# Routing of an expert mixture: the sample group's share moved one unit ahead, router gain and norm factor folded elsewhere, expert weights held back for the stores

## What is computed

```python
def rms_norm(x, g):
    xf = x.astype(F32)
    y = xf * lax.rsqrt(jnp.mean(xf * xf, axis=-1, keepdims=True) + NORM_EPS)
    return (y * g.astype(F32)).astype(x.dtype)

def expert_choice_moe(h, router_w, w_gate, w_up, w_down):
    n_tok = B * S
    cap = EC_CAPACITY * n_tok // N_EXPERTS
    xt = h.reshape(n_tok, D)
    aff = jax.nn.softmax((xt @ router_w).astype(F32), axis=-1)
    gates, idx = lax.top_k(aff.T, cap)
    xe = xt[idx]
    hid = jax.nn.silu(jnp.einsum('ecd,edf->ecf', xe, w_gate)) * jnp.einsum('ecd,edf->ecf', xe, w_up)
    ye = jnp.einsum('ecf,efd->ecd', hid, w_down) * gates[..., None].astype(h.dtype)
    y = jnp.zeros((n_tok, D), h.dtype).at[idx.reshape(-1)].add(ye.reshape(-1, D))
# in trunk, per layer:
    h = h + expert_choice_moe(rms_norm(h, ffn_norm[i]), router_w[i], ...)
```

## Time and profile before

| | |
|---|---|
| median of the runs | 2458.11 us |
| the profiled execution: time, span | 2456.45 us, 2454.8 us |
| TensorE busy, mean granted clock | 2367.5 us (96%), 0.985 |
| VectorE busy, ScalarE busy, GpSimd busy | 1742.6 (71%), 1337.0 (54%), 298.8 (12%) |
| experts' weight splits, 128x2048 | ScalarE 1913 ns, VectorE 2289 ns, 384 each |
| load of a chunk of `ret_w_in`, `ret_w_out`, 1 MB | 5.2, 5.1 us to landing |
| DMA rate in the slices of the experts | 389 to 395 GB/s |

### The profile page before, as it was taken

The page is one execution under the profiler, slowest core; times in us unless marked ns, Lnnn a source line. Parts: engine busy times, 40 slices in busy tenths (PEclk is TensorE's granted clock), DMA queues, the critical chain, the costliest instruction groups (busy, mean ns, idle before and its releaser), DMA issues.

```text
span 2454.8 us, 33887 instructions
## 1 busy us (share of the span) xinstructions
PE 2367.5 (96%) x11934; PEld 1934.6 (79%) x11934; DVE 1742.6 (71%) x1989; ACT 1337.0 (54%) x1454; POOL 298.8 (12%) x360
## 2 busy tenths in 40 slices
PE   8999999999979999999999999998889999999997
PEld 6878788687768888888878888886678888888876
DVE  6545455344679888888866677766578888888854
ACT  4223222222447777777764455444157777777762
POOL 1000000000111221112111101000111111121011
PEclk9999999999989999999999999998889999999999
DMA  6424324132499999999972533332599999999931
GB/s 235 132 72 126 108 96 149 59 107 72 157 345 395 389 392 392 394 389 390 388 193 56 134 102 99 93 93 73 170 339 393 392 394 390 389 392 392 356 125 43
DMA packets 210961, 577.27 MB, mean 235 GB/s; under 512 B 24384, under 2 KB 65856, under 8 KB 210752
## 3 DMA queue, kind: packets, MB, share of 16 engines
q1 hardware_dynamic: 193584, 526.35, 57.5%
q0 software_dynamic: 17296, 49.83, 8.0%
HBM read 547.80 MB, written 30.43 MB: 236 GB/s over the span
## 4 chain that ended last, share of the span: by engine, by line
PE 91%; DVE 3%; DMA 3%; issue 1%; ACT 1%; POOL 0%; SPq 0%; DVEq 0%; POOLq 0%; ACTq 0%
PE bank L1557 43%; PE bank L1443 38%; PE bank L1372 4%; PE bank L1380 4%; PE bank L1743 1%; PE bank L1725 1%; DMA rows_normed<-xn_late 1%; DVE d_parts L613 1%; DMA m_x<-rows_normed,idx_t 1%; DMA resid<-in_x_sample 0%; DMA rows_summed<-m_y,idx_out 0%; DMA raw<-in_ret_w_in 0%; DVE top_i L1946 0%; DVE m_at L1948 0%; DMA resid<-rows_summed 0%
## 5 line engine op out<-in xcount | busy, mean ns | idle before, releaser
L2080 DVE TENSOR_TENSOR w_parts<-wt,w_parts 128x2048 fp32r<-128x2048 f32 x384 | 874.5, 2289 | 133.7 <-ACT w_parts L1133 125.3
L1133 ACT CAST w_parts<-wt 128x2048 fp32r<-128x2048 f32 x384 | 734.2, 1913 | 195.0 <-PE bank L1557 184.4
L1557 PE MATMUL bank<-w_parts,m_xt 128*128 128x512 f32 x2976 | 689.0, 390 | 2.1 <-ACT m_y L1191 2.1
L1557 PEld LDWEIGHTS bank<-w_parts,m_xt 128*128 128x128 f32 x2976 | 556.1, 188 | 117.2 <-issue 2.9
L1443 PE MATMUL bank<-d_parts,xt 128*128 128x512 f32 (+1 forms) x1872 | 388.0, 364 | 4.4 <-DVE d_parts L613 4.4
L1557 PE MATMUL bank<-w_parts,m_hidt 128*128 128x512 f32 x1632 | 382.7, 394 | 2.8 <-DVE m_hidt L2072 2.8
L1443 PEld LDWEIGHTS bank<-d_parts,xt 128*128 128x128 f32 x1872 | 316.0, 190 | 62.3 <-issue 7.4
L1557 PEld LDWEIGHTS bank<-w_parts,m_hidt 128*128 128x128 f32 x1632 | 306.1, 189 | 66.0 <-issue 3.3
L604 ACT CAST d_parts<-raw 128x512 fp32r<-128x512 f32 (+1 forms) x168 | 183.3, 1107 | 245.5 <-PE bank L1443 237.4
L613 DVE TENSOR_TENSOR d_parts<-raw,d_parts 128x512 fp32r<-128x512 f32 (+1 forms) x168 | 215.5, 1296 | 134.8 <-ACT d_parts L604 134.3
L1443 PE MATMUL bank<-xt,d_parts 128*128 128x256 f32 (+1 forms) x1536 | 284.1, 340 | 7.0 <-DVE xt L1803 2.9
(11 more groups left out here) (184 smaller groups left out, 2035.6 us busy)
## 6 DMA issues: line engine op xcount, KB each, us to landing
wt<-in_exp_w_gate SPq DMA_DIRECT2D x128, 1024.0 KB, 14.2
wt<-in_exp_w_up SPq DMA_DIRECT2D x128, 1024.0 KB, 13.1
wt<-in_exp_w_down SPq DMA_DIRECT2D x128, 1024.0 KB, 13.3
raw<-in_ret_w_in SPq DMA_DIRECT2D x32, 1024.0 KB, 5.2
raw<-in_na_w_in SPq DMA_DIRECT2D x24, 1024.0 KB, 5.4
raw<-in_ret_w_in SPq DMA_DIRECT2D x32, 512.0 KB, 4.5
raw<-in_ret_w_out SPq DMA_DIRECT2D x16, 1024.0 KB, 5.1
raw<-in_ple_w_gate SPq DMA_DIRECT2D x8, 1024.0 KB, 8.1
```

The costliest lines, as they stand in the source:

```text
L1133: nc.scalar.copy(w_parts[c % RING][:, 0, :], wt[:, place // 2, place % 2 * 2048:place % 2 * 2048 + 2048])\
L1557: last = nc.tensor.matmul(b[:, :], lhs[x][:, 2 * k + j, :], w[:, part, j, f * HALF:(f + 1) * HALF], start=(k == j == 0 and x == part == 0) ...
L2080: v.tensor_tensor(w_parts[c % RING][:, 1, :], wt[:, k // 2, k % 2 * 2048:k % 2 * 2048 + 2048], w_parts[c % RING][:, 0, :].bitcast(F32), AL ...
```

## The change

1. The units end (2,S) (3,S) (3,P) (2,P), so that the last two are prompt units, and a fifth strip is needed (`strips`). All that the sample's routing had in the last unit now lies in the first of the two (`ROUTED`), except `scaled` of its tiles and most of `eight_best`, which are spread over both.
2. The router's columns are transposed from `resid` instead of the normed rows (`norm_columns`, `added_up`). The gain is multiplied into the router's weights once (`rw_gain`, `rw_scaled`), and the row's norm factor is applied as the scale of the exponential (one call for each tile instead of one for each group). `scaled` is still made, for the rows that experts gather, but later.
3. High and low part of the router's weights lie side by side (32 columns), so that two products per tile of the width give all four combinations, 16 products instead of 24. The sum of the two halves is made when they are brought back into tiles, by a product with `two`, two identity matrices above one another.
4. `moe_loads` waits before chunk 6 for the prompt's stores of normed rows too.
5. `keep_busy` of 20 now stands ahead of the prompt's router products in both layers. In layer 1 the order of output products and routing is another, and so are places in memory.

The diff, cut:

```diff
-UNITS = [(0, 0), (0, 1), (1, 0), (1, 1), (2, 0), (2, 1), (3, 1), (3, 0)]
+UNITS = [(0, 0), (0, 1), (1, 0), (1, 1), (2, 1), (3, 1), (3, 0), (2, 0)]
 LAST = len(UNITS) - 1
+ROUTED = LAST - 1
...
+def strips(u):
+    return sum(new_head(k) for k in range(u + 1))
...
-OUT_ORDER = ["out20", "out30", "out21", "out31", "out40", "norm2", "out41", "norm3", "out50", "norm4", "out51", "out00",
-             "norm5", "out10", "lg1", "out01", "lt1", "aff1", "out11", "norm0", "norm1"]
+OUT_ORDER = ["out20", "out30", "out21", "out31", "out40", "norm2", "out41", "norm3", "out50", "out51", "norm4", "norm5",
+             "out00", "lg1", "lt1", "out10", "aff1", "out01", "out11", "norm0", "norm1"]
...
+        def added_up(eng, n, t):
+            for f in range(2):
+                if n == 1:
+                    drained(eng, "ret", ("out", LAST, t, f) if t < 2 else ("out", ROUTED - 1, t - 2, f))
+                else:
+                    drained(eng, "naout", ("out", t, f))
...
+                    sp.dma_start(rw_gain[:].rearrange("p l t -> p (l t)"), ffn_columns).then_inc(late_in, 16)
...
                     if c == 6:
                         sp.wait_ge(sample_out[l], 16 * 4)
+                        sp.wait_ge(rows_out[l], 16 * 2)
...
+            nc.gpsimd.tensor_tensor(two[:, :], ident[0:2 * EXPERTS, 0:EXPERTS], ident[0:2 * EXPERTS, EXPERTS:2 * EXPERTS],
+                                    ALU.add).then_inc(ident_set, 1)
...
             for u in range(len(UNITS)):
-                if u == LAST:
+                if u == ROUTED:
                     for t in GROUP_TILES[1]:
                         root(1, t)
+                if u == LAST:
                     stored_group(0, 1)
...
             def exponents(l, g):
+                n = 1 + 3 * l
                 act.wait_ge(moe_sub[l], 2 - g)
-                x = m_lg[l][:, GROUP_TILES[g][0]:GROUP_TILES[g][-1] + 1, :]
-                nc.scalar.activation(x, x, ACT.Exp).then_inc(moe_exp[l], 1)
+                act.wait_ge(norm_rs[n], nth(n, GROUP_TILES[g][-1]))
+                for t in GROUP_TILES[g]:
+                    nc.scalar.activation(m_lg[l][:, t, :], m_lg[l][:, t, :], ACT.Exp, scale=rstd[:, t:t + 1])\
+                        .then_inc(moe_exp[l], 1)
...
             for t in range(2):
+                norm_high(1, t)
+            for t in range(2):
                 squares(1, t)
-            for t in range(2):
-                norm_high(1, t)
...
             def norm_columns(n, tiles):
                 for t in tiles:
-                    pe.wait_ge(norm_rows[n], nth(n, t))
+                    if n == 0:
+                        pe.wait_ge(norm_rows[n], nth(n, t))
+                    else:
+                        added_up(pe, n, t)
+                    rows = normed(n, t) if n == 0 else resid[:, t, :]
...
-                part_products([rw_parts[k][:, l, :, :] for k in range(2)], lambda k, m, j: xt[k][:, j, first:first + n],
-                              route_phase(l, g), [("lg", g)], DT, lambda m: slice(0, EXPERTS), True, True, m=EXPERTS)
+                for j in range(DT):
+                    for k in range(2):
+                        last = nc.tensor.matmul(b[0:2 * EXPERTS, 0:n], rw_parts[:, l, j, :], xt[k][:, j, first:first + n],
+                                                start=(j == k == 0), stop=(j == DT - 1 and k == 1))
...
-                    last = nc.tensor.transpose(b[:, k * EXPERTS:(k + 1) * EXPERTS], m_at[l][g][:, k * P:(k + 1) * P],
-                                               ident[0:EXPERTS, 0:EXPERTS])
+                    last = nc.tensor.matmul(b[:, k * EXPERTS:(k + 1) * EXPERTS], m_at[l][g][:, k * P:(k + 1) * P],
+                                            two[:, :], start=True, stop=True)
...
             def mixture(l):
+                keep_busy(f"route{l}", ("lg", 0), 20)
                 logits(l, 0)
...
-            keep_busy("route0", ("n1", 0, 0), 20)
             norm_columns(1, (0, 1))
...
```

198 lines of the change are left out of this document (109 added, 89 removed).

## The result

| | before | after |
|---|---|---|
| median of the runs made together | 2458.44 us (2456.77 to 2460.53) | 2463.18 us (2457.17 to 2466.88) |
| ratio, 95% interval | | 1.002 (1.0011 to 1.0029) |
| the profiled execution: time, span | 2456.45, 2454.8 us | 2466.88, 2465.2 us |
| TensorE busy, mean granted clock | 2367.5 us (96%), 0.985 | 2369.6 us (96%), 0.984 |

The changed kernel is slower by 4.7 us, 0.2% of the time. Mind the two profiled executions: that of before is on the fast side of its runs, that of after is the slowest of its own, so the spans differ by 10.4 us where the medians differ by 4.7. The same file run and profiled again (e1) has a span of 2463.0.

The account below looks back on a forecast made before the run. TensorE, busy 96%, was taken as the bound, with VectorE never idle in the routings. Layer 0 +6.3 -3.2, layer 1 -2.8 -3.1, together -2.8: 2455.3 us, range 2446 to 2463 (the forecast's own 2452 to 2459).

Parts of the forecast that it names:

- The sign of the whole: Whole kernel: faster, with layer 0 at +3.1 us and layer 1 at -5.9, together -2.8 us.
- What bounds the kernel: Retention: TensorE waits for almost nothing, so added work shows once TensorE waits; in both routings VectorE is never idle.
- Part 1, the four waits: Layer 0's prompt pair: TensorE waits at o0 0.4, o1 1.75, v0 2.15 and the gate 2.05 us.
- The 8 products: Layer 0 before T: 8 of 24 router products removed, worth -1.8 us.
- Part 1, the clock: Layer 0's prompt pair: only the gate's pause drops the granted clock, +1.7 us; bounds 0 and 8.
- my rival, four falls: Layer 0's prompt pair: the clock falls in all four pauses, +6 us, 2461.3, or 2463 with late gathers; chance 0.13.
- T of layer 0: End of layer 0's last output product (T): 6.3 us later, from waits less removed products +4.6 and clock +1.7.
- Part 2: Layer 0 from T, the last output product's end, to M, the first expert product: 31.8 us, a gain of 3.2.
- The gather under the held chunks: Both routings: the gather meets weight chunks 6 to 9, held for the prompt's stores; +3.3 us each.
- The first rival: Both routings: the gather isn't slowed by the held chunks, -3.3 us twice, 2448.7 us; chance 0.27.
- Part 3 ahead of T: Layer 1 before T: 8 products -1.8, affinities' wait of 1.65 gone, tile products' wait +0.67; sum -2.8 us.
- Part 3 behind T: Layer 1, T to M: indices at T+22.7, store wait gone by itself, M at T+36.6, a gain of 3.1 us.

Follow-up runs that it names:

- e3: Changed kernel with VectorE's order altered in layer 0's last two units, no eight_best ahead of o0's split or between centred and gated; 2457.89 us, 1.0000.
- e5: Changed kernel with the fifth strip, for the last prompt unit, worked out for 384 columns and not 896; 2459.93 us, 1.0008.
- e9: Changed kernel with the unit order of before, all of the sample's routing in the last unit; 2457.41 us, 0.9994.
- e2: Changed kernel without the wait for the prompt's stores ahead of weight chunk 6; 2464.34 us, 1.0026.
- e6: Changed kernel with layer 1's prompt stores sent from SP, one transfer for each grid row of a tile; 2464.08 us, 1.0019.
- e12: Changed kernel with the filling transposes of e11 alone, 102 ahead of the gathered rows and 11 ahead of the first expert product; 2457.18 us, 0.9997.
- e7: Changed kernel with the edits of e3, e5 and e6 together; 2458.12 us, 0.9998.
- e8: e7 with 80 instead of 36 filling transposes ahead of the gathered rows in each layer; 2457.93 us, 0.9995.
- e11: e7 with 102 filling transposes ahead of the gathered rows and 11 more before the first expert product; 2449.92 us, 0.9966.
- e4: Kernel before with the hold alone, chunks 6 to 9 waiting for the prompt's stores of normed rows; 2459.3 us, 1.0005.
- e10: e9 with layer 1's prompt stores sent row by row as in e6; 2455.8 us, 0.9988.
- e13: Kernel before with filling transposes, 66 in layer 0, 86 in layer 1, and 11 ahead of the first expert product; 2454.33 us, 0.9987.

## Why the prediction was wrong

**The sign of the whole is wrong, by two mis-sized terms and one left out.** The sum had one fall of the clock in the prompt pair, and there were two; it had layer 1's last store landing ahead of the indices, and it landed behind them; and it had nothing for the tile products with `two`. Point by point.

- *What bounds the kernel.* Right: each change of VectorE's list in the prompt pair moved T (e3, e5, e9).
- *Part 1, the four waits.* Right in place and order, and 0.75 too small in sum. Idle times of 0.20, 1.46, 1.82 and 2.78 us stand in the rows above. Counted as the forecast counted them, from start to start, they are 0.37 (6.20 for 5.83), 1.75 and 2.11 (7.20 and 7.56 for 5.45), and 2.86 at the gate (679.46 less the end of the gates at 674.05, less the 2.55 of the earlier trace rows). That is 7.1, where 0.4, 1.75, 2.15 and 2.05 were forecast, 6.35. The pause at the gate itself came as worked out (2.78, for 29.8 - 26.95 = 2.85); the 0.8 more lies in the transposes behind it, 2.6 us for 1.7, with the clock down. The 8 products gave 1.85.
- *Part 1, the clock.* **This term failed.** I wrote that the pauses up to 2.15 us "may escape", and took one fall at 1.7. The size of a fall was right: 12.8 and 12.9 us for 48 products, where e5 and e9 took 11.2 and 11.3. But the pause of 1.82 at v0 made the clock fall as well, so there were two falls, 3.2 us for 1.7. It was not chance, for it fell in all six profiles with 1.8 us at v0 (after, e1, e2, e3, e6, e12), and in none with 0.3 (e5, e7, e8, e11). The earlier trace rows had both kinds, a fall after 2.05 us at 1764 and none after 2.07 at 686, and I followed the kinder one. Of my rival, four falls, two happened. That its time, 2461.3 to 2463, lies by the measured 2463.2 is luck: the rest of the way to that time came from the stores and the tile products.
- *Part 1, left out.* The tile products with the matrix `two` contract over 32 rows instead of 16 and take 1.06 us for the sample's tiles, where the kernel before took 0.42: +0.65 in each layer. I had only asked whether they would wait.
- *T of layer 0.* 4.6 + 1.7 forecast. Measured, 7.1 + 3.2 + 0.65 - 1.85 = 9.1 of the 9.3 us by which T is later behind the third group; e9 puts the spread alone at 10.5. The other 0.7 of the 10.0 is the start of that execution: 1.3 us later, of which 0.55 was made up ahead of the third group.
- *Part 2.* The router started at T+5.8, as forecast. The indices, forecast for T+18.4, were there at T+19.0 (T+24.9 before). The last store landed at T+19.5, not T+17, 11.2 us after its issue; the gather went out at T+20.4 for T+19.5, and some 0.5 of that is the wait for the store, for in before it followed the indices by 1.0. It took 9.8 us for 9.4. M is at T+33.1 for T+31.8.
- *The gather under the held chunks.* Right: 9.8 and 10.2 us in after, 9.7 and 9.8 in e1, 8.2 and 10.5 in e4; without the hold 6.0 in layer 1 and 8.4 in layer 0 (e2). The first rival, a gather that isn't slowed, is refuted. What the text cited of the Trainium skill (DMA: Bandwidth & Descriptors, the section on queues, rings and completion order) holds all the same: the two queues took turns packet by packet, and got half each. From 720 to 721 us of after's trace, while the gather (q0) and a weight chunk (q1) moved:

```profile
q0 software_dynamic: 36, 0.15, 50.2%
q1 hardware_dynamic: 36, 0.15, 49.7%
```

What failed was my estimate of 1 us from it, for it left out when the gather's data starts. In e2's layer 1, alone, its first bytes moved 3.6 us after its issue and it landed 2.4 us later; in after's layer 0, 6.3 us after its issue and 3.4 later. So half the rate cost 1.0 us, as by the rule, and the later start of the data 2.7. Why the data starts later under load, these runs don't show.
- *Part 3 ahead of T.* -2.2 for -2.8; the difference is the tile products again. The router ran at full clock (2.03 us for its 16), and the second transposes waited 2.1 us, as forecast. The wait at the affinities is gone.
- *Part 3 behind T.* **The second term that failed.** Indices were ready near T+23 for T+22.7. "The wait of before for the store is gone by itself" is false: its store landed in 16.6 us (13.3 in e1) with the weights held back, and the gather went out at T+27.8 (T+24.6). I had read the 23.9 us of the earlier trace rows as the load of the weights beside it and assumed layer 0's store time. The load was 7 to 11 us of it; the other 13 to 17 remain with the load held back, and e6's, by row and from SP's queue, moved 389 GB/s. M is at T+37.3 to T+41.0 in the five profiles with this code, T+38.9 in the median; forecast T+36.6.
- *Behind M.* I took nothing to change there. The first products of the experts took 13.8 and 13.3 us for 12.5 and 12.9, and a fall of the clock at the embedding came in after's profile and not in before's, together 3 us in the profile. The second comes and goes with the execution (e10, above). Of the first, the profiles and e12 beside e13 say that 0.7 to 2.5 us may be the change's.

Medians: +4.7 instead of -2.8 is 7.5 us. The clock in the pair gives 1.5 of it, the waits there 0.75, the tile products 1.3, layer 0's indices, store and gather 1.3, layer 1's store 2.3 in the median of its five profiles (0.7 to 4.4), the clock at M 0.7 to 1.7. That is 7.9 to 8.9 with the median for the store, so nothing large is missing, but how the store of layer 1 and the clock at M share the rest is not settled, and neither is what the later start is worth.

What slows the stores of layer 1 stays open too, since e6 changed shape, size and queue at once. The Trainium skill (DMA: Bandwidth & Descriptors, section "Why a DMA increments its semaphore by 16 and not by 1") has the number of engines as the largest up to 16 that divides the slowest dimension of both sides. The same section names an exception, that some direct copies from GpSimd's queue run on all 16. By the rule, a store whose slowest dimension is 4 would run on 4 of 16. The trace doesn't settle this. The mean busy share of the 16 engines was 0.88 and 0.75 while the stores moved 152 and 132 GB/s, but four of them were in flight, and four times four would be all 16; from 1796 to 1797, near the end of the last, the share was 0.24. The packets say this much. From 1784 to 1796 us of after's trace:

```profile
DMA packets 1189, 1.83 MB, mean 153 GB/s; under 512 B 742, under 2 KB 742, under 8 KB 1189
```

Three in five of its packets are under 512 B and hardly carry anything, against 272 of 879 in e6 from 1782 to 1791 us. But they are not the whole cause, for there is a stretch without them, from 1786 to 1788:

```profile
DMA packets 96, 0.39 MB, mean 197 GB/s; under 512 B 0, under 2 KB 0, under 8 KB 96
q0 software_dynamic: 96, 0.39, 98.1%
```

The engines were busy for 98% of it and moved 197 GB/s, where weights (above, from 1800 to 1804) moved 413 at 1.01. So packets of 4 KB themselves took twice as long and more, and what makes them slow I have not shown.

## What to carry to other kernels

Price a pause of the bounding engine with the clock's fall behind it: here a wait of 1.8 us (2.1 from start to start) cost 3.7 with it, and 1.1 us less on VectorE with 0.4 less on ScalarE (e5) gave back 3.2. Work moved into an engine's slack belongs behind the operations that the bounding engine waits for next: the same list in another order (e3) was worth 5.3 us. Where a transfer is late under load, read its rate with the load gone before counting on it to be quick, and where the bounding engine must idle ahead of its main work, let it run fillers right up to that work: this was the largest gain of all, 8.2 us on e7 (e11), 6.0 on the changed kernel (e12), and 3.5 on the kernel before (e13), so it doesn't need the change.

## What the hardware did that I had not expected

- The granted clock fell to its lower level of 1.2 GHz behind every pause of 1.8 us at v0 (six profiles) and came back 3.4 us later in after, 6.8 at the gate; 48 products took 12.8 and 12.9 us instead of 11.2. At the embedding, it fell in 19 of 32 cases: after some pauses of 1.9 to 3.8 us and not after others of 1.5 to 2.9. Behind the pause of 2.09 us at layer 1's second transposes it fell in e1, e3, e6 and e11 and not in after. Which one it will be I can't say from these runs.
- At M the clock was low for 5.6 us after work had begun again (until 731 in after, M at 725.34; 2.8 us in before), and filling that stopped 2.8 us short of the gathered rows only moved the fall onto the products (e8, 13.8 us). Filling without a gap kept it at 1.00 (11.2 us).
- The prompt's strided stores from GpSimd's queue moved 132 to 152 GB/s with the DMA engines 75 to 88% busy and nothing beside them; the same rows from SP's queue, a transfer for each grid row, ran at 389.
- An indirect gather of 96 rows beside a weight chunk got half the bandwidth (50.2% for 49.7% from 720 to 721), and its first bytes moved 6.3 us after its issue, for 3.6 alone (e2).
